# Hybrid decoder step, sparse expert layers: row transfers counted by parity, a seventh row buffer, another order on GpSimd, and the sparse body placed first

## The reference, cut to what matters

```python
D_MODEL = 1024; N_EXPERTS = 16; N_EXPERT_GROUPS = 4; TOP_K = 2; D_EXPERT = 256
scores = jax.nn.sigmoid(h @ w_router)                       # T x 16
# best group of four experts, then the two best experts of that group
gates  = sum over the two of one_hot(idx) * (score / sum of the two scores)
y = jnp.zeros_like(h)
for e in range(N_EXPERTS):
    he = jax.nn.silu(h @ w_gate[e]) * (h @ w_up[e])         # 256 wide
    y = y + gates[:, e:e + 1] * (he @ w_down[e])
x = _layernorm(alpha * x + y, g, b)                         # the post norm
```

## Time and profile before

| | |
|---|---|
| time, median of 3 runs | 1180.44 us (1177.11 to 1183.77) |
| time of the profiled execution | 1178.25 us |
| its span | 1176.4 us |
| PE busy | 1027.6 us (87%) |
| DVE, ACT, POOL busy | 513.9, 376.1, 199.7 us |
| sparse part of layer 0, first to last PE instruction | 209.0 to 390.7 us |
| sparse part of layer 1, first to last PE instruction | 966.2 to 1151.7 us |
| transfers in the span | 217.87 MB, mean 185 GB/s |

### The profile page before, as it was taken

How to read it: one execution, slowest core, us unless ns; L and a number is a source line. 1 busy time by engine, 2 the same in 40 slices (tenths; PEclk the granted TensorE clock), 3 DMA queues, 4 the chain that set the end, 5 groups by cost and what they waited for, 6 DMA issues and landing times.

```text
span 1176.4 us, 25885 instructions
## 1 busy us (share of the span) xinstructions
PE 1027.6 (87%) x10322; PEld 682.0 (58%) x10322; DVE 513.9 (44%) x1303; ACT 376.1 (32%) x943; POOL 199.7 (17%) x236
## 2 busy tenths in 40 slices
PE   9999994898879399999999999999999929988791
PEld 3686452665446157777788887556555526644450
DVE  1670325122435404489546654765524341224353
ACT  1101113243445323323244332354421213433451
POOL 0010001122445200000211111411000011244341
PEclk9999996798889799999999998999999959988896
DMA  9755008799895332132322242574641379998820
GB/s 327 294 53 223 37 19 328 252 370 362 286 360 166 111 129 108 38 101 76 93 73 71 78 136 73 185 298 163 248 157 70 132 254 330 368 322 296 310 85 27
DMA packets 82721, 217.87 MB, mean 185 GB/s; under 512 B 13637, under 2 KB 54645, under 8 KB 64240
## 3 DMA queue, kind: packets, MB, share of 16 engines
q1 hardware_dynamic: 65184, 155.38, 36.6%
q0 software_dynamic: 17408, 60.73, 16.2%
HBM read 206.28 MB, written 46.89 MB: 215 GB/s over the span
## 4 chain that ended last, share of the span: by engine, by line
PE 64%; DMA 16%; issue 7%; DVE 6%; POOL 3%; ACT 2%; SPq 0%; POOLq 0%; DVEq 0%; ACTq 0%
DMA parts<-work,part_row 11%; PE bank L1320 9%; PE bank L1591 9%; PE bank L1499 5%; PE bank L1416 5%; PE bank L1690 4%; DMA parts<-acc,part_row 3%; PE bank L1562 2%; PE bank L1525 2%; PE bank L1440 2%; PE bank L1944 1%; PE bank L1969 1%; PE bank L1331 1%; PE bank L1345 1%; PE bank L1311 1%
## 5 line engine op out<-in xcount | busy, mean ns | idle before, releaser
L1320 PE MATMUL bank<-ring,cat 128*128 128x512 f32 x256 | 112.6, 594 | 1.3 <-ACT cat L2123 1.3
L1591 PE MATMUL bank<-xT,ring 128*128 128x288 f32 x448 | 110.9, 407 | 0.0
L1591 PEld LDWEIGHTS bank<-xT,ring 128*128 128x128 f32 x448 | 84.6, 190 | 23.8 <-issue 1.1
L1416 PE MATMUL bank<-ring,work 128*32 128x128 f32 (+1 forms) x1344 | 87.4, 326 | 1.7 <-DVE work L2564 1.7
L2614 DVE SCALAR_TENSOR_TENSOR acc<-acc,stat,lnp 96x1024 f32<-96x1024 f32 x24 | 30.7, 1279 | 127.5 <-POOL stat L1131 127.3
L1320 PEld LDWEIGHTS bank<-ring,cat 128*128 128x128 f32 x256 | 47.5, 190 | 57.2 <-issue 57.2
L1416 PEld LDWEIGHTS bank<-ring,work 128*32 128x32 f32 (+1 forms) x1344 | 60.4, 125 | 27.7 <-issue 17.4
L1499 PE MATMUL bank<-xT,ring 128*128 128x288 f32 x256 | 63.1, 407 | 0.0
L1499 PEld LDWEIGHTS bank<-xT,ring 128*128 128x128 f32 x256 | 48.3, 190 | 13.5 <-issue 0.4
L2109 ACT COPY work<-bank 32x256 f32<-32x256 f32 x120 | 43.4, 362 | 9.9 <-PE bank L1440 8.4
L1398 PE MATMUL bank<-const,work 96*128 96x96 f32 x192 | 24.4, 280 | 24.3 <-DMA work<-xkept,idx 24.2
(11 more groups left out here) (473 smaller groups left out, 2074.7 us busy)
## 6 DMA issues: line engine op xcount, KB each, us to landing
ring<-in_stream_dram SPq DMA_DIRECT2D x61, 1024.0 KB, 8.2
work<-in_stream_dram SPq DMA_DIRECT2D x16, 1024.0 KB, 8.9
cat<-in_stream_dram SPq DMA_DIRECT2D x16, 1024.0 KB, 10.7
by_batch<-in_pages_dram SPq DMA_DIRECT2D x128, 128.0 KB, 2.4
x<-in_stream_dram SPq DMA_DIRECT2D x12, 1024.0 KB, 9.8
xT<-in_stream_dram SPq DMA_DIRECT2D x12, 1024.0 KB, 9.5
lnp<-in_ln_dram POOLq DMA_DIRECT2D x4, 1024.0 KB, 10.7
xkept<-x POOLq DMA_DIRECT2D x8, 512.0 KB, 2.9
```

The costliest lines, as they stand in the source:

```text
L1320: i = pe.matmul(bank(n)[0:ROWS[tile], :], cat[:, k, tok(tile)], slot(w[k // 4], 4, 512)[:, k % 4, :], start=(k == 0), stop=(k == KC - 1))
L1416: i = pe.matmul(by_half[rows * q:rows * q + rows, :, to:to + width], xgT[:, e % 2, k, at:at + rows], w[:, :, width * q:width * q + width], ...
L1591: i = pe.matmul(bank(n + s)[:, 0:nn], slot(w, KC, 256)[:, k, P * (m % 2):P * (m % 2) + P], xT[:, k, a:a + nn], start=(k == 0), stop=(k == ...
```

## The change

- `part_kept` and `part_back` become two semaphores each, one for even and one for odd experts. `keep_part(e)` now waits for keep e-2, and `fetch_part(e)` for fetch e-2.
- There are seven row buffers instead of six. The seventh lies where the third `yS` buffer was; `yS` has two buffers now. A gather of expert e waits for the keep (and, where it has one, the norm) of expert e-7.
- The round of POOL for expert e is now: gather e+3, keep e-2, fetch e, then norm step and final write of e-2. The fetch stands one expert nearer to its use.
- On all five engines the sparse body is the `If` body (`flag < 1`) and the dense body the `Else` body.
- POOL no longer waits for the landing of the final writes; SP still does.
- The `widened` and `fast_step` semaphores are folded into others, and the step count of DVE is levelled by a constant at the end of the sparse body.

```diff
-NXG = 6
+NXG = 7
-NYS = 3
+NYS = 2
...
-        part_kept = [sem(f"part_kept{k}") for k in range(LAYERS)]
-        part_back = [sem(f"part_back{k}") for k in range(LAYERS)]
+        part_kept = [[sem(f"part_kept{k}{i}") for i in range(2)] for k in range(LAYERS)]
+        part_back = [[sem(f"part_back{k}{i}") for i in range(2)] for k in range(LAYERS)]
...
                 def part_landed(e):
-                    pool.wait_ge(part_kept[layer], 16 * (e + 1))
+                    pool.wait_ge(part_kept[layer][e % 2], 16 * (e // 2 + 1))
+
+                def gather_ahead(e):
+                    take(pool, ejob(layer, e - EARLY_ROWS, "T1"))
+                    if e >= NXG:
+                        part_landed(e - NXG)
+                    if e - NXG >= NG:
+                        pool.wait_ge(finished, final_count(layer, e - NXG))
+                    gather_rows(e)
 
                 def keep_part(e):
-                    if e > 0:
-                        part_landed(e - 1)
+                    if e > 1:
+                        part_landed(e - 2)
...
                 def fetch_part(e):
                     take(pool, ejob(layer, e, "T1"))
                     part_landed(e - NG)
-                    if e > NG:
-                        pool.wait_ge(part_back[layer], 16 * (e - NG))
+                    if e - 2 >= NG:
+                        pool.wait_ge(part_back[layer][e % 2], 16 * ((e - NG) // 2))
...
-                with pool.If(flag > 0):
+                with pool.If(flag < 1):
+                    pool.wait_ge(acc_and_gates, NT * (layer + 1))
+                    for e in range(EARLY_ROWS, NXG - 1):
+                        gather_ahead(e)
+                    ln_params(2 * layer + 1)
+                    pool.wait_ge(slots_weighed, layer + 1)
+                    for e in range(2, N_EXP + 2):
+                        if NXG - 1 <= e + 3 < N_EXP:
+                            gather_ahead(e + 3)
+                        if e - 2 < N_EXP - NG:
+                            keep_part(e - 2)
+                        if NG <= e < N_EXP:
+                            fetch_part(e)
+                        if NG <= e - 2:
+                            invert(e - 2)
+                            write_final(e - 2)
+                with pool.Else():
                     ln_params(2 * layer + 1)
                     for i in range(EARLY_ROWS):
                         pool.wait_ge(xg_loaded[layer][i], rows_in(i))
-                with pool.Else():
-                    for e in range(2, N_EXP + 2):
-                        if NG <= e + 1 < N_EXP:
-                            fetch_part(e + 1)
-                        if NXG <= e + 3 < N_EXP:
-                            part_landed(e + 3 - NXG)
-                            if e + 3 - NXG >= NG:
-                                pool.wait_ge(finished, final_count(layer, e + 3 - NXG))
-                            gather_rows(e + 3)
-                        if e - 2 < N_EXP - NG:
-                            keep_part(e - 2)
-                        if NG <= e - 2:
-                            invert(e - 2)
-                            write_final(e - 2)
-                    landed_finals(pool, layer)
...
-                with pe.If(flag > 0):
+                with pe.If(flag < 1):
+                    own_tokens(layer)
+                with pe.Else():
                     every_expert(layer)
-                with pe.Else():
-                    own_tokens(layer)
```

More of the change, by code:

```diff
@@ L812, in program @@
         row_rstd = stat[:, 466:468]
-        o += NYS * D_MODEL
+        xg.append(work[:, o + NYS * D_MODEL:o + NYS * D_MODEL + D_MODEL])
+        assert len(xg) == NXG
+        o += (NYS + 1) * D_MODEL
         hgS = view(work, o, PART)
@@ L1059, in _ @@
                     ahead = [BLOCK_AT["oin", q] for q in (8, 7)] if layer == 0 else []
-                    with sp.If(flag > 0):
-                        for m in [*rest, *sorted(ahead)]:
-                            load(m, BLOCKS[m - NSLOT][1])
-                        if layer == LAYERS - 1:
-                            for tile in range(NT):
-                                sp.wait_ge(ln_done, (2 * LAYERS - 1) * NT + tile + 1)
-                                sp.dma_start(outs["x"][tok(tile), :], x[0:ROWS[tile], tile, :]).then_inc(x_stored, 16)
-                            sp.wait_ge(x_stored, 16 * NT)
-                    with sp.Else():
+                    with sp.If(flag < 1):
                         take(sp, ejob(layer, 0, "T1"))
@@ L1081, in _ @@
                                 sp.dma_start(x[0:ROWS[tile], tile, :], xnext[tok(tile), :]).then_inc(tile_loaded[tile], 16)
+                    with sp.Else():
+                        for m in [*rest, *sorted(ahead)]:
+                            load(m, BLOCKS[m - NSLOT][1])
+                        if layer == LAYERS - 1:
+                            for tile in range(NT):
+                                sp.wait_ge(ln_done, (2 * LAYERS - 1) * NT + tile + 1)
+                                sp.dma_start(outs["x"][tok(tile), :], x[0:ROWS[tile], tile, :]).then_inc(x_stored, 16)
+                            sp.wait_ge(x_stored, 16 * NT)
                     n = rest.stop + len(ahead)
@@ L1113, in keep_part @@
                         in_=xg[e % NXG][0:CAP, :], in_offset=None,
[L1114 removed]
+                        bounds_check=T - 1, oob_is_err=False).then_inc(part_kept[layer][e % 2], 16)
                 def fetch_part(e):
@@ L2043, in mixture @@
                 flag = is_crowded(act, layer)
-                with act.If(flag > 0):
-                    for e in range(N_EXP):
-                        for m in range(2):
-                            for s, (a, nn) in enumerate(SPLITS):
-                                n = job(f"{L}e{e}", 4 * m + 2 * s)
-                                take(act, n)
-                                give(act.activation(hg[:, e % 2, m, a:a + nn], bank(n)[:, 0:nn], ACT.Silu), n)
-                    for tile in range(NT):
-                        spread(2 * layer + 1, tile)
-                with act.Else():
+                with act.If(flag < 1):
                     act.wait_ge(slots_found, 2 * layer + 2)
@@ L2111, in mixture @@
                             give(i, n)
+                with act.Else():
+                    for e in range(N_EXP):
+                        for m in range(2):
+                            for s, (a, nn) in enumerate(SPLITS):
+                                n = job(f"{L}e{e}", 4 * m + 2 * s)
+                                take(act, n)
+                                give(act.activation(hg[:, e % 2, m, a:a + nn], bank(n)[:, 0:nn], ACT.Silu), n)
+                    for tile in range(NT):
+                        spread(2 * layer + 1, tile)
             def gate(m):
@@ L2517, in mixture @@
+                step.count[0] = steps_before
+                with dve.Else():
                     dve.wait_ge(idx_named, layer + 1)
@@ L2662, in mixture @@
-                step.count[0] = steps_after
+                    assert step.count[0] == steps_before + GENERAL_STEPS
             dve.memset(stat[:, :], 0.0).then_inc(zeroed, 1)
```

218 lines of the change are left out of this document (101 added, 117 removed).

## The result

| | before | after |
|---|---|---|
| time, median | 1182.02 us (4 runs) | 1132.80 us (4 runs, 1130.75 to 1134.82) |
| ratio of the times | 1 | 0.959, 95% interval 0.955 to 0.963 |
| time and span of the profiled execution | 1178.25, 1176.4 us | 1130.75, 1129.0 us |
| loop, turn of expert 3 to turn of 15, layer 0 | 135.79 us | 121.50 us |
| the same, layer 1 | 140.12 us | 122.11 us |

The change is worth 47 us of span. The forecast was 1116 us, with 1108 to 1142 as its range: the time lies inside, 17 us above the forecast and above 1124, the upper end that the forecast gave for its own mechanism.

A forecast was written before the change was run, and what follows sets the result against it. It took PE, held to POOL's pace by late rows in the sparse loops, and DVE's time behind the branch as the bounds. Terms -24.8 - 29.1 - 4.35 - 9.1 + 1.0 + 4.0 = -62.3 from 1178.25 gave 1116 us, range 1108 to 1142.

The forecast's parts named there:

- The round of POOL: Sparse loops: keep, gather and fetch wait for a keep two rounds old, so no landing stays; a round takes 8.7 us.
- 9.25 us per expert to the end: Sparse loops, experts 3 to 15: PE keeps its unstalled pace, winning 24.8 us in layer 0 and 29.1 in layer 1.
- both fit with 3 us or more: Row transfers: gathers have 15.4 us against a longest landing of 12.2, fetches some 15 against 9.8.
- the prediction's own signs: Wrong if PE waits over 5 us per layer, POOL's rounds exceed 9.25, the branch gap stands, or a new gap appears.
- The stream of weights: Sparse loops: weights fall back 1.5 us per expert, within a 29 us lead; 2 us per layer allowed, late rows included.
- The branch: Ahead of the sparse loops: sparse body first removes DVE's code fetching, winning 4.35 us in layer 0, about 9.1 in layer 1.
- The end: After the last final write: the moved jump costs 1.0 us, POOL's dropped wait counts 0 because SP holds it too.
- A: Sparse loops: the stream of weights replaces the keeps and PE stalls 16 us per layer; 1124 to 1144 us, chance 0.15.
- B: Sparse loops: POOL becomes the pace through longer issues, rounds of 10.3 us; 1132 us, chance 0.11.
- C: Behind the branch: the time stays, not being fetched code, so 13.4 us less is won; 1129 us, chance 0.08.
- D: POOL's round: no gain, something else such as DVE's sum sets it; 1178 us or so, chance 0.02.
- E: DMA engines: more transfers in flight move less in all; at 250 GB/s 48 us slower, 1226 us, chance 0.02.

The follow-up runs named there:

- the first experiment: The kernel before with only the sparse body placed first on all five engines: 1169.29 us, ratio 0.991.
- the first two experiments: The kernel before with only the bodies exchanged, 1169.29 us; the changed kernel with the dense bodies first again, 1141.43 us.
- two pieces: The changed kernel with each 1024 KB weight block loaded by two transfers of 512 KB: 1127.31 us, ratio 0.955; run again, 1129.06 us, 0.955.

## Why the prediction was right, and where it was 17 us off

**The round of POOL.** Right. No keep's landing is in the round, two rounds lie between a keep and who waits for it, and the experiments without parity and with six buffers each bring back such a wait; parity alone leaves the fetch's. The line that the seventh buffer costs nothing holds too, but it said nothing of its worth: without it 1149 us instead of 1128 to 1133.

**9.25 us per expert to the end.** Right for eight of the twelve steps, wrong for the last four. The step that failed is "both fit with 3 us or more", which took the longest landings of the trace before (12.2 and 13.4 us) as the landings after. Those were landings in a kernel that stalled, and its stalls let the backlog run down: before, the DMA share is 0.93 from 276 to 308 us and 0.83 from 308 to 332, now 1.02 in both. The slack of the gather came out right, 15.4 us predicted and 15.3 in the trace, but by luck. The final write at 293.71 is that of expert 4, so the gather behind it would be the one for expert 10, whose rows are used two turns after the turn of 283.47, not three; and the 12.3 us to it came from a round that already ran late. In the changed kernel the gather goes out 3.2 us after a turn, and its rows are used two turns later: 18.5 - 3.2 = 15.3. The landing was 16.9 us at the gather for expert 12 and up to 20.7 later in that layer. By the prediction's own signs this part was wrong: PE waits 8.5 and 9.2 us per layer for rows, over the 5 it named, and POOL's rounds pass 9.25 us (9.33 from the gather of expert 11 to that of 12, then 9.48 and 11.4).

**The stream of weights.** The backlog that this part forecast was there: 4.03 MB in 10.8 us at 373 GB/s, 1.5 us behind per expert. In size it was 11.2 us at 359 GB/s, so 2.0 behind. The 21 us by the growth of the landings before was too low, since these came from the kernel that stalled; the 28 is nearer to the 32.2 measured. But it was booked against the weights' lead of 29 us alone. One backlog makes all transfers on the 16 engines late, and the row transfers, with 15 us of slack, were the first to have none left. The weights came up to 32.2 us after their request, more than the 29 of lead at PE's old pace, and kept nobody waiting, since PE's own rounds had grown to 12 us. In numbers the term "2 us per layer for this and for rows that come late", 4.0 in sum, is the one mis-sized: it measured (121.50 - 111.0) + (122.11 - 111.0) = 21.6. Half the bytes of weights took it to nothing, and seven eighths to 10.2.

**The branch.** Right in cause. In layer 1 9.1 us were forecast and 9.1 measured, which is partly luck: from the issue of the first gather to the first turn of rows it was 16.2 us before (953.21 to 969.41) and is 6.4 now (936.00 to 942.40), 9.8 us less. The landing of the gather did not hold PE up, as the forecast had it; the gather took 6.0 us instead of 7.1. The other 0.7 us went ahead of the branch, where the change does nothing: from layer 1's first turn to that gather it was 0.8 us longer. In layer 0 5.5 against 4.35: PE's slot lists came 4.2 us earlier, and its clock went up earlier too. The windows of 212 to 216 and 216 to 220 us, before and then after, have it at 0.50 in both, the lower level of 1.2 GHz, and then at 0.79 and at 1.00, the upper one of 2.4 GHz:

```profile
212.00:216.00 4.00, 3.15 (x19) 2.39 (x20) 0.89 (x4) 1.76 (x2) 0.95 (x1) 0.50 0.30 72
216.00:220.00 4.00, 4.00 (x22) 2.54 (x20) 0.00 (x0) 0.00 (x0) 0.00 (x0) 0.50 1.00 416
```

```profile
212.00:216.00 4.00, 4.00 (x42) 2.55 (x42) 0.00 (x0) 0.00 (x0) 0.00 (x0) 0.79 1.01 407
216.00:220.00 4.00, 4.00 (x85) 3.46 (x76) 1.47 (x3) 1.86 (x6) 0.86 (x1) 1.00 0.74 212
```

The jump that now ends the sparse body costs nothing that shows. The trace also names queues that carry instructions. In the gap of layer 0, 201.66 to 206.01, these are their packets and MB before:

```profile
q8 instruction: 1, 0.02, 1.9%
q14 instruction: 2, 0.02, 1.8%
```

In the run with the dense bodies first again they are there in its gap too, in the same numbers; in the changed kernel neither queue moved a packet from 200 to 211 us, nor in the run with only the bodies exchanged from 195 to 207. So code was fetched in the gap; the rows do not say for which engine. The rule of the Trainium skill (Runtime: NRT & Kernel Launch, Instruction fetch mechanics) that a taken branch whose target is outside a window of two blocks stalls for the fetch agrees with all of this: the gap goes and comes with the place of the body, and in the first experiment nothing else was changed. Whether DVE's target lay outside that window was not counted.

**The end.** Forecast +1.0 us for the jump and 0 for the dropped wait of POOL; measured -3.0, and the run with the wait put back shows that it was the wait. "SP holds it too" was no reason: a second engine that waits for the same landing costs about 3 us at the end of the program. How it does so the traces don't show.

**The sum.** Forecast -62.3, measured -47.4. Of the 14.9 between them 17.6 are the loops, -4.0 the end, -1.15 the clock in layer 0, and 2.45 the two stretches behind the loops (1.75 and 0.7), which the forecast had left as they were. That 1132.8 lies in the range is owed to the room left for A and B; the range of the sum alone ended at 1124.

**The rivals.** A had the cause and the wrong victim: the byte supply takes the place of the keeps, and 1124 to 1144 holds the time, but PE never waits for weights in the changed kernel. With two pieces it does, at the same time in sum. B's 1132 is the measured number by chance. POOL's instructions did lengthen to 1.87 to 2.06 us for three gathers, as B said, but POOL did not fall behind before PE had to wait: the gather of the round stands 3.34 us after PE's turn at 273.68 (277.02), and 3.45 us after the one at 301.43 (304.88). C falls by the first two experiments, D by the result. E's collapse did not come: with two keeps in flight the engines move 362 GB/s instead of 373 from 228 to 276 us, 3% less.

## What to carry to other kernels

Where a counter can't tell which transfer landed, count the waits for the youngest transfer in a round: order, semaphore and buffer each may hold one, and a change pays in full only when the last of them goes. Landing times read from a kernel that stalls are too short for the one that doesn't: forecast them as the backlog, bytes against the full engines' rate, and hold that one backlog against every stream on these engines, the one with the least slack first. Splitting transfers moved the wait from one stream to another here and was no cure for bytes.

## What was not expected of the hardware

- A row transfer of 0.2 to 0.3 MB took 20 us to land where weight blocks of 1 MB took 25.9 to 32.2. With half the weights' bytes gathers took 8.8 us at most.
- A request for a transfer can take longer to issue: three of POOL's gathers in a layer 1.87 to 2.06 us instead of 0.96 (layer 0), SP's requests for 512 KB up to 5.78 us instead of 0.33. Full engines are not all of it, since the gathers from 304.88 on took 1.01 us with the engines as full and landings later still; the cause stays open.
- The wait of one more engine for the last transfers made the end of the program about 3 us longer (13.1 to 13.5 us against 10.1 to 10.2, over fourteen traces), though another engine waits for the same.
